# Heads' statistics per chunk, the scaling signalled in two parts, low parts at second half steps, and the last turn in halves, in a hybrid decoder step on one core

## What is computed

```python
h = rmsnorm(x, norm_g)
p = h @ w_in                                   # 12,296 columns: inputs of four branches and their gates
o_a = silu(a_z) * (a_b * dwconv3(a_c * a_u))
o_r = silu(r_z) * head_norm(retention(rotary(r_q), rotary(r_k), r_v))
o_c = silu(c_z) * silu(layernorm(dwconv31(glu(c))))
o_m = silu(m_z) * head_norm(sigmoid(m_o) * mlstm(m_q, m_k, m_v, m_i, m_f))
y = x + (sum_n sigmoid(g_n) * (o_n @ w_br[n])) @ w_out
return rmsnorm(y, final_g), states
```

## Time and profile before

| | us |
|---|---|
| median of three runs | 1487.86 (1487.59 to 1489.18) |
| the profiled execution, its own time | 1487.17 |
| its span, first to last instruction | 1485.4 |
| TensorE busy | 1462.8 (98%) |
| VectorE busy | 903.5 (61%) |
| GpSimd busy | 579.8 (39%) |
| ScalarE busy | 534.6 (36%) |

### The profile page before, as it was taken

The page is one execution under the profiler, slowest core; times in us unless marked ns, Lnnn a source line. Parts: engine busy times, 40 slices in busy tenths (PEclk is TensorE's granted clock), DMA queues, the critical chain, the costliest instruction groups (busy, mean ns, idle before and its releaser), DMA issues.

```text
span 1485.4 us, 26706 instructions
## 1 busy us (share of the span) xinstructions
PE 1462.8 (98%) x10318; PEld 1422.4 (96%) x10318; DVE 903.5 (61%) x1746; ACT 534.6 (36%) x1111; POOL 579.8 (39%) x456
## 2 busy tenths in 40 slices
PE   9999999999999999899999999999999999999998
PEld 8999999999999999899999999999999999999786
DVE  6455252555666655687977878867656324885542
ACT  6343433333344345333333333334453422220221
POOL 1000000000010021787767767776777844662100
PEclk9999999999999999999999999999999999999999
DMA  8120212112021121322133222232322476755221
GB/s 314 43 86 32 85 59 87 63 55 91 29 91 62 58 80 50 105 91 90 59 102 94 87 76 72 73 101 87 95 81 101 153 234 202 235 159 147 105 86 73
DMA packets 65526, 148.36 MB, mean 100 GB/s; under 512 B 7976, under 2 KB 36920, under 8 KB 65272
## 3 DMA queue, kind: packets, MB, share of 16 engines
q1 hardware_dynamic: 58008, 120.06, 25.0%
q0 software_dynamic: 6192, 22.27, 4.2%
q10 hardware_dynamic: 1200, 4.33, 0.7%
HBM read 110.99 MB, written 35.64 MB: 99 GB/s over the span
## 4 chain that ended last, share of the span: by engine, by line
PE 86%; DVE 5%; ACT 2%; DMA 2%; issue 1%; POOL 1%; SPq 0%; DVEq 0%; ACTq 0%; POOLq 0%
PE bank L1203 11%; PE bank L1205 11%; PE bank L1204 11%; PE bank L1154 9%; PE bank L1156 9%; PE bank L1155 9%; PE bank L1221 4%; PE bank L1222 4%; PE bank L1223 4%; PE bank L1415 1%; PE bank L1417 1%; PE bank L1416 1%; PE sums_ps L1311 1%; PE sums_ps L1326 1%; PE sums_ps L1330 1%
## 5 line engine op out<-in xcount | busy, mean ns | idle before, releaser
L1154 PE MATMUL bank<-h_hi,w_hi 128*128 128x352 f32 x960 | 319.6, 333 | 1.4 <-POOL w_lo L1802 1.2
L1156 PE MATMUL bank<-h_hi,w_lo 128*128 128x352 f32 x960 | 309.0, 322 | 0.0
L1155 PE MATMUL bank<-h_lo,w_hi 128*128 128x352 f32 x960 | 308.3, 321 | 0.0
L1203 PE MATMUL bank<-h_hi,t_hi 128*128 128x264 f32 x896 | 256.1, 286 | 0.0
L1204 PE MATMUL bank<-h_lo,t_hi 128*128 128x264 f32 x896 | 254.6, 284 | 0.0
L1205 PE MATMUL bank<-h_hi,t_lo 128*128 128x264 f32 x896 | 254.1, 284 | 0.0
L1802 POOL TENSOR_TENSOR t_lo<-stage,t_hi 128x512 fp32r<-128x512 f32 x144 | 195.5, 1360 | 139.8 <-ACT t_hi L1457 139.7
L1203 PE MATMUL bank<-c_hi,t_hi 128*128 128x264 f32 x672 | 191.3, 285 | 2.4 <-DVE part L2073 2.4
L1205 PE MATMUL bank<-c_hi,t_lo 128*128 128x264 f32 x672 | 191.0, 284 | 0.0
L1204 PE MATMUL bank<-c_lo,t_hi 128*128 128x264 f32 x672 | 190.3, 283 | 0.0
L1154 PEld LDWEIGHTS bank<-h_hi,w_hi 128*128 128x128 f32 x960 | 180.5, 188 | 3.1 <-POOL w_lo L1802 1.5
(11 more groups left out here) (368 smaller groups left out, 2887.9 us busy)
## 6 DMA issues: line engine op xcount, KB each, us to landing
stage<-in_wa SPq DMA_DIRECT2D x64, 512.0 KB, 3.4
piece<-g_rows SPq DMA_DIRECT2D x96, 176.0 KB, 2.7
stage<-in_wg SPq DMA_DIRECT2D x32, 512.0 KB, 3.7
g_rows<-sgt SPq DMA_DIRECT2D x120, 132.0 KB, 1.9
o_raw<-o_rows SPq DMA_DIRECT2D x16, 528.0 KB, 6.8
stage<-in_wb SPq DMA_DIRECT2D x32, 256.0 KB, 2.8
xt<-in_xT SPq DMA_DIRECT2D x6, 704.0 KB, 12.7
o_rows<-zs POOLq DMA_DIRECT2D x8, 528.0 KB, 3.0
```

The source lines that it names most:

```text
L1154: pe.matmul(out, hi, h_hi[:, k, tok(b)], start=(k == 0), stop=False)
L1155: pe.matmul(out, hi, h_lo[:, k, tok(b)], start=False, stop=False)
L1156: mm = pe.matmul(out, lo, h_hi[:, k, tok(b)], start=False, stop=(k == KD - 1))
L1203: pe.matmul(out, hi, a_hi(k), start=(first and k == 0), stop=False, skip_group_check=True)
```

## The change

- `("pr", hd)` stands in the step of `("bs2", hd)`, one step earlier.
- A low part is put behind the next *second* half step of a block (`s[3]`), not behind the next half step.
- The low part of `("keep", 5)` is VectorE's, ahead of its turns; the last wait of TensorE for these weights is for two low parts.
- Head 0's first scores wait for `gate_dve` 8; its first product with the values waits for 17.
- `bn_stats` of a retention head's eight chunks stand in `b`, behind `num_done`; `pn` keeps the samples' only.
- `norm_done` rises twice per head, behind chunk 3 and behind the samples; each half of TensorE's transposes waits for its own.
- In the last turn, squares, scaling and stores are done in two halves of 512 columns; SP issues one store, ScalarE the other.
- In `free`, `or not before` is added.

```diff
         t = [[("a", hd, 0)]]
         t += [[("b", hd, c - 1), ("a", hd, c)] for c in range(1, CH)]
-        t += [[("b", hd, CH - 1), ("as", hd)], [("bs1", hd), ("pn", hd)], [("bs2", hd)],
-              [("pr", hd)], [], [("pt", hd, 0)], [("pt", hd, 1)]]
+        t += [[("b", hd, CH - 1), ("as", hd)], [("bs1", hd), ("pn", hd)], [("bs2", hd), ("pr", hd)],
+              [], [], [("pt", hd, 0)], [("pt", hd, 1)]]
...
         if before != "g":
-            free = free[1:] if free[0] == 0 else free
+            free = free[1:] if free[0] == 0 or not before else free
...
             plan_out.append(s)
-            if s[0] == "blk":
+            if s[0] == "blk" and s[3]:
                 while lows:
...
-    return item[0] == "plain" and item[1] not in (0, 2)
+    return item == ("keep", 5) or item[0] == "plain" and item[1] not in (0, 2)
...
+            sp.wait_ge(y_done, 9)
+            sp.dma_start(y[TP - P:TP, 0:512], yo[0][:, 0:512]).then_inc(y_out[0], 16)
...
                     if hd == 0:
-                        pe.wait_ge(gate_dve, 17)
+                        pe.wait_ge(gate_dve, 8)
...
                     if hd:
                         pe.wait_ge(pt_used, 3 * hd)
+                    else:
+                        pe.wait_ge(gate_dve, 17)
...
-                pe.wait_ge(norm_done, hd + 1)
                 if half == 0:
                     pe.wait_ge(upd_done, 2 * hd + 2)
                     for g, t in ((0, tb), (1, pb)):
+                        pe.wait_ge(norm_done, 2 * hd + 1 + g)
...
                         if i == 0 and q == 1 and k == 2:
 
+                            low_parts(pe, NSPL - 2)
                             low_parts(pe, NSPL - 1)
...
-                own.wait()
-                act.sem_inc(norm_done, 1)
+                    if c in (3, CH):
+                        own.wait()
+                        act.sem_inc(norm_done, 1)
...
+                if i == 8:
+                    for q in range(2):
+                        half = slice(512 * q, 512 * q + 512)
+                        act.wait_ge(y_sum, 2 * i + q + 1)
+                        act.activation(squares[:, half], yt[0][:, half], ACT.Square, accum_out=ss[:, 6, q:q + 1]).then_inc(y_sq, 1)
+                        act.wait_ge(y_sq, i + q + 1)
+                        if q == 0:
+                            act.activation(ss[:, i, 0:1], ss[:, 6, 0:1], ACT.Identity, scale=1.0 / D, bias=eps[:, :]).then_inc(y_half, 1)
+                            act.wait_ge(y_half, 1)
+                    act.activation(ss[:, i, 1:2], ss[:, 6, 1:2], ACT.Sqrt, scale=1.0 / D, bias=ss[:, i, 0:1]).then_inc(y_act, 1)
+                    act.wait_ge(y_done, i + 2)
+                    act.dma_start(y[r0:r0 + n, 512:D], yo[0][:, 512:D]).then_inc(y_out[0], 16)
+                    break
...
                 dve.sem_inc(num_done, 1)
+                if hd >= 4:
+                    own(dve.bn_stats(stat[:, c, :], rt[:, c, 0:P]))
...
-                for c, r in rows:
+                for c, r in rows if hd < 4 else rows[CH:]:
                     own(dve.bn_stats(stat[:, c, :], rt[:, c, 0:P]))
...
+            low(NSPL - 1)
             dve.wait_ge(late_in, 32)
...
+                if i == 8:
+                    for q in range(2):
+                        half = slice(512 * q, 512 * q + 512)
+                        dve.scalar_tensor_tensor(yo[0][:, half], yt[0][:, half], ss[:, i, 1:2], fgb[:, half], ALU.mult,
+                                                 ALU.mult).then_inc(y_done, 1)
+                    continue
```

More of the change, by code:

```diff
@@ L849, in hybrid_step @@
         y_act = sem("y_act")
+        y_half = sem("y_half")
         y_rec = sem("y_rec")
@@ L1593, in a @@
                     if c == 0 and hd:
-                        act.wait_ge(norm_done, hd)
+                        act.wait_ge(norm_done, 2 * hd)
                     own(act.activation(so[0:r, c, :], tb[0:r, 2 * P:3 * P], ACT.Sigmoid))
@@ L1760, in _ @@
                     fin(i + 2)
-                act.wait_ge(y_sum, 2 * i + 2)
                 if i:
@@ L1764, in _ @@
                 r0, n = by_turn[i] * P, rows_of(i)
+                if i == 8:
[11 more added lines that the diff above has]
+                    break
+                act.wait_ge(y_sum, 2 * i + 2)
                 act.activation(squares[0:n, :], yt[i % 2][0:n, :], ACT.Square, accum_out=ss[0:n, i, 0:1]).then_inc(y_sq, 1)
@@ L1769, in _ @@
                 act.dma_start(y[r0:r0 + n, :], yo[i % 2][0:n, :]).then_inc(y_out[i % 2], 16)
-            act.wait_ge(y_out[0], 16 * 5)
+            act.wait_ge(y_out[0], 16 * 6)
             act.wait_ge(y_out[1], 16 * 4)
```

## The result

The changed kernel is slower: 1496.49 us (four runs, 1496.06 to 1496.73) against 1488.43 for the kernel before on the same chip, a ratio of 1.0055 (95% interval 1.0039 to 1.0071), some 8 us. The forecast was 1488.9 with a range to 1491.6. The profiled execution has a span of 1494.3 us against 1485.4.

The account below looks back on a forecast made before the run. TensorE's busy time bounds the kernel, so only its waits can change the time. Terms sum to +1.3 us (losses 1.93, 2.9, 0.2, 0.9; gains 1.23, 0.45, 1.5, 0.6, 0.8); from 1487.6 to 1488.9, range 1485.2 to 1491.6.

Parts of the forecast that it names:

- What bounds the kernel; the places where TensorE waits: Whole kernel: TensorE is busy 1462.8 of 1485.4 us, so the time can only change where it stands still.
- head 7's last transpose: Head 7: TensorE's wait of 2.5 us before it mostly goes, gaining some 2 us, expected lost again 30 us later.
- Opening: Unit 3's first matmul: the low part now stands behind the copy of unit 2's last block, +1.93 us.
- first scores: Head 0's first scores: TensorE no longer waits 1.62 us for the last gate mask before transposing, -1.23 us.
- last turn: Tail behind the last matmul: squares and stores in halves, -0.8 us, with ends -0.4 and -1.1.
- the low part of `keep` 5: Last output weights: low part moves from GpSimd (2.39 us) to VectorE (1.23), TensorE's wait goes, -0.6 us.
- Second-to-last chunks: Heads 3 to 6: the low part between two half steps with attention delays the next scores, +2.9 us in all.
- Heads 0 and 3: Transposes: head 0's earlier scaling nets -0.45 us; head 3's low part leaves the reciprocal's way, -1.5 us.
- from there the chain is unbroken: Behind head 7: low part, load, sums and combinations make TensorE wait for the partial sum 0.9 us later, +0.9.
- rival C: Behind head 7's low part: the load lands later, slower; at 2.5 us more the time is 1491.4; chance 0.17.
- Rival D: Unit 3's 1.9 us standstill lowers TensorE's clock, a block costs 3.8 us more, at least 1492.7; chance 0.03.
- the 0.1 of heads 1 and 2: Heads 1 and 2: last unit's low part ready some 0.1 us before TensorE asks; 0 set, 0.5 each if missed.

Follow-up runs that it names:

- the first run: The changed kernel with the low parts back behind the next half step, all else of the change kept: 1484.26 us, 0.9976 of the kernel before.
- the run with the later loads: The changed kernel with GpSimd's two loads (history into ext, and ahist) issued behind the four h_lo subtractions instead of ahead: 1495.80 us, 1.0056 of the kernel before.
- the runs without the stall: Two runs of the changed kernel: GpSimd's four h_lo subtractions replaced by memsets to zero, 1491.17 us; or held until all four combinations are done and split, 1492.15 us.

## Why the prediction was wrong

*What bounds the kernel; the places where TensorE waits*: right. Every wait forecast is there, and within 0.5 us of its size but for two: head 7's last transpose, of which 1.4 us stayed, and the partial sum.

*Opening, first scores, last turn*: right (1.8, 1.3 and 0.8 where 1.9, 1.2 and 0.8 stood), and the low part of `keep` 5 took 0.7 off (the first turn's matmul at 1380.68 moved by 10.4 us, the last matmul by 9.7), 0.6 said. A store of 256 KB lands in 2.0 to 2.1 us, 0.5 to 0.6 less than one of 512 KB, where 0.4 to 0.5 stood.

*Second-to-last chunks*: right in kind, 0.9 us short in sum. The low part costs a chunk 0.65 in head 3 and about 1.0 in each of heads 4 to 6, of which the table of waits shows only 0.38 and 0.68. In head 6 the next wait, 0.33, comes on top; it stands in the kernel without the moved low parts too (0.32). For head 3 the prediction's own count, 1.0 less 0.47 spare, gives 0.5, and its sum has 0.4.

*Heads 0 and 3*: the sizes were near (0.2 for 0.45; 1.4 for 1.5). Head 3's reason held; what the sum did not say is that `pr` a step earlier would have brought the gain by itself, as the first run showed.

*"from there the chain is unbroken ... That is 0.9 later than before. Whatever TensorE wins in between, it waits for the partial sum 0.9 later"*: this is the step that failed. The low part's end, the load and the sums on GpSimd came as said (+1.2 us up to the first combination; rival C did not happen, GpSimd's first sum starts 3.96 us behind its low part). But I carried the chain's lengths over as constants. The four combinations are 15.1 us in the earlier trace rows's execution only because of what lay beside them there; their own work is twelve times 0.71. I looked at what the chain waits for, not at what runs beside its links, though the rows of 0.71 and 1.69 for one and the same operation stood in the trace of before. GpSimd's work beside them hangs on TensorE, so TensorE's own gain of 1.8 us at head 7 counted against it. Measured: +4.2 for +0. With the `h_lo` held back, and so without the stall, the kernel takes 1492.15, still above the range: 1.5 of the clock, 0.9 of the chunks and 0.8 of the level (1488.4, where 1487.6 was taken) make up the difference to the forecast.

*Rival D*, the clock: priced at unit 3's 1.9 us, where nothing fell in the changed kernel's profiled execution. In the run with the later loads it did fall there, behind the same 1.75, and cost 1.8, not the 3.8 of a whole block. And the prediction had a standstill of above 4 us before the partial sum and gave it no price. There the clock fell behind 8.64, and also behind the 4.14 and 4.20 of the runs without the stall, for 1.5 us each: a second term that stood at nothing without a reason. Range and chances had no case in which two of the kernel's chains slide against each other; the thin ends that I took in (C, and the 0.1 of heads 1 and 2) did not happen.

*What stays open*: why the one operation waits for two subtractions of GpSimd, where in most rows the two engines take turns. It happened in the profiled execution of all five kernels in which `h_lo` that are ready stand directly behind the two loads, beside a combination (4.02 to 4.04 each), and in none of the others. Neither half does it: five subtractions in one row without the loads left it at 1.8 and below, the loads without subtractions behind them at 0.71. A run without the loads but with two ready subtractions that start at the same moment wasn't made.

## What to carry to other kernels

Where two engines read the same memory side by side, as VectorE and GpSimd here, an operation can have two durations or more, and a chain's length is no constant. Ask of every step that moves, and of every wait that goes, what it will then run beside, above all where one chain goes by a load and the other by the engine that you make faster. A wait on the busiest engine can be what keeps two others apart: taking 2.5 us away made the kernel 6 us slower here, until the subtractions nobody needed yet were put behind those that were needed. Before a sum is trusted, list the places where the same instruction shows two durations.

## What was not expected of the hardware

- VectorE's `tensor_tensor` with both inputs in SBUF (128x528): 0.71 us alone, 1.56 to 1.85 beside an addition or subtraction on GpSimd, which then mostly takes 1.75 instead of 1.29, and 4.02 to 4.04 where two of them stand directly behind two load issues, though it is shown to start ahead of the first. Beside GpSimd's load issues (0.94 and 0.55 us) and its memsets: 0.71. Additions with one input in PSUM keep their 0.43 beside GpSimd's work.
- TensorE's clock does not follow the length of a wait alone. In the profiled executions it fell to its lower level within or behind every standstill from 2.49 us up but one: behind 2.85 (twice), 4.14, 4.20, 4.36 and 7.26 to 8.64 us, and behind 2.49 in one execution of two with the same waits. Of the shorter ones, 1.75 to 2.0 us, it fell behind four (1.75 at unit 3 in one of six executions, 1.95 at head 0 in two, 2.0 at the start in one) and stayed up behind ten; behind shorter ones it never fell. In the units a fall lasted for some 10 to 19 matmuls at 0.29 instead of 0.16 apart and cost 1.5 to 2.4 us; the one behind 8.6 us cost 1.5. The Trainium skill (TensorE: Matmul & The Clock Gate, Part 1) says that idling brings such a fall; the trace agrees here.
